# Recurrent branch's projections with 512-column operands, their halves added by VectorE

## The reference, cut to what matters

```python
u = rms_norm(h, norm1_g[l])
proj = (u @ w_in[l]).astype(jnp.float32)
q, k, v, z = jnp.split(proj, [ATTN_WIDTH, 2 * ATTN_WIDTH, 3 * ATTN_WIDTH], axis=-1)
...
prev = jnp.pad(z, ((0, 0), (1, 0), (0, 0)))[:, :-1]
z = z + (prev - z) * shift_mix
```

## Time and profile before

| | us |
|---|---|
| median of 3 runs | 3240.96 (3236.51 to 3246.12) |
| the profiled execution's own time | 3238.11 |
| its span | 3236.3 |
| TensorE busy | 3172.6 |
| VectorE busy | 1626.7 |
| ScalarE busy | 1484.4 |
| GpSimd busy | 2500.0 |

### The profile page before, as it was taken

How to read it: one execution, slowest core, us unless ns; L and a number is a source line. 1 busy time by engine, 2 the same in 40 slices (tenths; PEclk the granted TensorE clock), 3 DMA queues, 4 the chain that set the end, 5 groups by cost and what they waited for, 6 DMA issues and landing times.

```text
span 3236.3 us, 62096 instructions
## 1 busy us (share of the span) xinstructions
PE 3172.6 (98%) x22458; PEld 2810.5 (87%) x22458; DVE 1626.7 (50%) x2999; ACT 1484.4 (46%) x1981; POOL 2500.0 (77%) x1117
## 2 busy tenths in 40 slices
PE   8999999999999999998999999999999999999999
PEld 7888888988888888997789998888888888888888
DVE  3268646522222322497565958876612664157600
ACT  5466544544444444545454554443444335433433
POOL 6821255888888888888587887898898889887887
PEclk9999999999999999999999999999999999999999
DMA  6554204555555555653355555555565555555555
GB/s 223 185 168 127 82 20 134 192 188 189 190 189 189 184 188 185 199 164 124 111 183 170 182 182 174 175 182 175 173 197 188 176 177 186 188 182 175 175 195 169
DMA packets 158763, 553.22 MB, mean 171 GB/s; under 512 B 18000, under 2 KB 24288, under 8 KB 158496
## 3 DMA queue, kind: packets, MB, share of 16 engines
q1 hardware_dynamic: 152208, 541.37, 51.2%
q0 software_dynamic: 3248, 6.77, 0.9%
q10 hardware_dynamic: 3168, 3.15, 0.3%
HBM read 548.33 MB, written 2.88 MB: 170 GB/s over the span
## 4 chain that ended last, share of the span: by engine, by line
PE 66%; POOL 15%; issue 10%; DVE 5%; ACT 2%; DMA 1%; POOLq 0%; ACTq 0%; DVEq 0%; SPq 0%
PE ps L769 37%; PE ps L771 19%; POOL wl L604 15%; PE ps L757 6%; PE ps L1028 1%; DVE wl L1912 1%; PE ps L1340 1%; DVE from_u L2521 1%; ACT wh L1448 0%; DMA xT<-x 0%; PE ps L836 0%; DVE arena L1991 0%; DMA raw<-w_z 0%; ACT under_u L1615 0%; PE ps L955 0%
## 5 line engine op out<-in xcount | busy, mean ns | idle before, releaser
L604 POOL TENSOR_TENSOR wl<-raw,wh 128x1024 fp32r<-128x1024 f32 x980 | 2367.2, 2424 | 482.8 <-ACT wh L1448 480.5
L1448 ACT ACTIVATE wh<-raw 128x1024 fp32r<-128x1024 f32 (+1 forms) x1034 | 1084.2, 1053 | 1415.5 <-PE ps L771 1182.3
L769 PE MATMUL ps<-uhl,wh 128*128 128x512 f32 x3200 | 1119.7, 395 | 12.1 <-DVE uhl L1894 11.7
L771 PE MATMUL ps<-uhl,wl 128*128 128x256 f32 x3200 | 893.0, 279 | 0.0
L769 PEld LDWEIGHTS ps<-uhl,wh 128*128 128x128 f32 x3200 | 600.8, 188 | 149.4 <-DVE wl L1912 10.3
L771 PEld LDWEIGHTS ps<-uhl,wl 128*128 128x128 f32 x3200 | 604.3, 189 | 0.1
L757 PE MATMUL ps<-uhl,wh 128*128 128x256 f32 x2976 | 549.4, 287 | 3.4 <-POOL wl L604 1.2
L769 PE MATMUL ps<-ehl,wh 128*128 128x512 f32 x1536 | 551.4, 400 | 0.3 <-POOL wl L604 0.3
L757 PEld LDWEIGHTS ps<-uhl,wh 128*128 128x128 f32 x2976 | 469.0, 193 | 11.4 <-issue 6.1
L1903 DVE TENSOR_REDUCE ps<-ps 128x256 f32<-128x512 f32 x168 | 117.5, 699 | 634.3 <-PE ps L771 633.5
L771 PE MATMUL ps<-ehl,wl 128*128 128x256 f32 x1536 | 431.6, 281 | 0.0
(11 more groups left out here) (367 smaller groups left out, 3625.7 us busy)
## 6 DMA issues: line engine op xcount, KB each, us to landing
raw<-w_u SPq DMA_DIRECT2D x256, 512.0 KB, 3.7
raw<-w_v SPq DMA_DIRECT2D x256, 512.0 KB, 3.7
raw<-w_gu SPq DMA_DIRECT2D x176, 512.0 KB, 4.3
raw<-w_down SPq DMA_DIRECT2D x80, 512.0 KB, 3.9
raw<-w_out SPq DMA_DIRECT2D x64, 512.0 KB, 3.9
raw<-w_z SPq DMA_DIRECT2D x54, 512.0 KB, 4.2
raw<-w_in SPq DMA_DIRECT2D x52, 512.0 KB, 4.2
raw<-w_qkv SPq DMA_DIRECT2D x48, 512.0 KB, 4.3
```

Source lines behind the costliest of these rows:

```text
L604: pool.tensor_tensor(wl[:, slot, 0:width], raw[:, slot, 0:width], wh[:, slot, 0:width].bitcast(F32), ALU.subtract).then_inc(lo_ready, 1)
L769: pe.matmul(bank(b).rearrange("p (n t) -> p n t", n=2), wh[:, slot, at], both, start=first and c == 0, stop=False, skip_group_check=True)
L771: ins = pe.matmul(bank(b)[:, 0:T], wl[:, slot, at], high, start=False, stop=last and c == kt - 1, skip_group_check=True)
L1448: act.activation(wh[:, slot, 0:width], raw[:, slot, 0:width], ACT.Copy).then_inc(hi_ready, 1)
```

## The change

The tiles of z are computed by `pair_tile`: a 512-column and a 256-column matmul for each chunk. VectorE adds the halves of the bank into a new buffer `ZS` in SBUF (two slots, in `misc`), as the first thing of its turn, ahead of the head's mask. ScalarE's scaled copy and VectorE's shifted product read `ZS`, not the bank. ScalarE waits for the new semaphore `z_sum` instead of for the end of the tile.

```diff
+        ZS = view(misc, 512, 2, T)
...
+        z_sum = sem("z_halves_added")
...
-                    tile(bank(c % 2)[:, 0:T], g, g % RING, uhc, ulc,
-                         (lambda: pe.wait_ge(u_ready, DT)) if c == 0 else
-                         (lambda: key_sums(WT - 1)) if c == 26 else None)
+                    pair_tile(c % 2, g, UHL, (lambda: pe.wait_ge(u_ready, DT)) if c == 0 else
+                              (lambda: key_sums(WT - 1)) if c == 26 else None)
...
-                    act.wait_ge(w_used, BASE["z"] + 2 * c + 2)
+                    act.wait_ge(z_sum, c + 1)
...
-                    act.activation(z_out(c), bank(c % 2)[:, 0:T], ACT.Identity, scale=keep[:, c:c + 1])\
+                    act.activation(z_out(c), ZS[:, c % 2, :], ACT.Identity, scale=keep[:, c:c + 1])\
...
             for c in range(29):
                 h = c - HEAD_LAG
+                if c < 27:
+                    dve.wait_ge(w_used, BASE["z"] + 2 * c + 2)
+                    if c >= 2:
+                        dve.wait_ge(z_ready, c - 1)
+                    add_halves(ZS[:, c % 2, :], c % 2).then_inc(z_sum, 1)
                 if 0 <= h < NH:
                     dve.wait_ge(sc_ps, h + 1)
...
-                    dve.scalar_tensor_tensor(out=late, in0=bank(c % 2)[:, 0:T - 1], scalar=prm("mix", c), in1=late,
+                    dve.scalar_tensor_tensor(out=late, in0=ZS[:, c % 2, 0:T - 1], scalar=prm("mix", c), in1=late,
```

## The result

The changed kernel takes 3245.12 us (median of 22 runs, 3240.61 to 3253.94) where the kernel before, on the same chip in turn with it, takes 3235.89 us (22 runs, 3231.01 to 3246.12). The ratio is 1.0031, with a 95% interval from 1.0025 to 1.0038: some 10 us slower, 8 to 12 us by the interval. The prediction had +9.5 us. Its absolute 3250.5 us lies 5.4 us higher because it started from the three runs shown, whose median is 5.1 us above that of the 22.

A forecast was written before the change was run, and what follows sets the result against it. VectorE together with ScalarE was taken to bound turns 5 to 18. -1.7 (TensorE) + 6.2 (adds) + 3.0 (last turn) + 2.0 (clock) = +9.5 us, a median of 3250.5 us, range 3241 to 3257.

The forecast's parts named there:

- VectorE sets the pace from turn 5 to 18, and two of three adds count: z stage: VectorE with ScalarE paces these turns; nine adds there push the chain, +6.2 us.
- The adds are hidden: Rival, chance 0.10: VectorE's idle time takes the adds in turns 6 to 18; +1.3 us, 3242.3 us.
- The size of an add: VectorE's reduction in the z stage: 0.69 us each, nine adds +6.2 us, lower bound within the mechanism 5.5 us.
- TensorE's gain of 1.7 us: z tiles 3 to 5 and 20, 21, 23, 24, 25: 0.21 us saved a tile on the chain, together -1.7 us.
- -11.8 us: Rival, chance 0.04: TensorE bounds the z stage, all 27 tiles count and slow-clock stretches vanish; 3229.2 us.
- 512-column matmuls much cheaper: Rival, chance 0.03: 512-column matmuls take 0.13 us instead of 0.23, eight tiles gain 13 us more; 3237.5 us.
- The last turn, +3.0: Turn 26: the add waits for the last tile ahead of the key norms, delaying the last bonus sums, +3.0 us.
- The clock, +2.0 with bounds -4.7 and +8: z stage: longer TensorE waits bring 1.2 GHz stretches in turns 10 to 16; turn 19 may give time back.
- no net loss: Rival, chance 0.17: waits pass without slowing TensorE's clock, or turn 19 repays; +7.5 us, 3248.5 us.
- every long wait halves the clock: Rival, chance 0.08: each long TensorE wait brings 1.2 GHz and each delay comes in full; +15.5 us, 3256.5 us.
- everything follows the chain: Behind the z stage: nothing waits for something else that would swallow a delay, so the +9.5 us arrives whole.
- the bound between no change and slower: Total time: a measurement tells about 0.3% from no change, 9.7 us; slower by more had chance 0.44.

The follow-up runs named there:

- pair, no add: Changed kernel without VectorE's adds; readers take the bank's first half, leaving a part out of z: 3238.58 us, ratio 0.9999 to the kernel before.
- adds only: Kernel before, three matmuls a chunk, plus the 27 reductions where the change has them, results unused: 3253.83 us, ratio 1.0037 to the kernel before.
- norms first: Changed kernel with the last key norms ahead of the last add in turn 26: 3246.54 us, ratio 1.0022 to the kernel before.
- turn late, again: The kernel of turn late, unchanged, timed and profiled a second time: 3234.49 us, ratio 0.9991 to the kernel before.
- turn late: Changed kernel reordered: adds behind the maxima, shifted product a turn later, exponentials before z's copy, earlier bank reuse, last norms before last add: 3238.82 us, ratio 0.9999.
- by turn: Changed kernel with 512-column matmuls and adds in turns 0 to 5 and 19 to 25, three matmuls a chunk elsewhere: 3239.84 us, ratio 1.0001.
- kept busy: Changed kernel with 16 unused matmuls ahead of the bonus sums of turns 10, 13, 16 and 19: 3248.27 us, ratio 1.0026.

## Why the prediction came out right, step by step

- **VectorE sets the pace from turn 5 to 18, and two of three adds count: right.** The period grows by 1.22 us with one add and by 1.20 more with two; without adds it is 26.70, and with the adds behind the maxima 26.33 us. *The adds are hidden* is refuted by that; in another place in the queue, behind the maxima, the time is that of before.
- **The size of an add: 0.61 us, not 0.69.** The prediction took the duration, 6.2 us for nine, and named the overlap of rows as its lower bound of 5.5; the lower bound holds: nine times 0.61 is 5.5 us, and 4.9 us of it are seen in the four periods. In this full queue an instruction costs the distance of starts and not its duration.
- **TensorE's gain of 1.7 us: mis-sized, some 1.2.** Tiles 3 to 5 gain 0.38 us (0.65 expected), turns 22 to 25 take 21.85 us instead of 22.37, 0.52 (0.63 expected), in pair, no add 0.40; so 0.13 to 0.17 us a tile instead of 0.21. In the times it is below what can be measured. The two rivals that had TensorE decide (-11.8 us, and 512-column matmuls much cheaper) are refuted: adds only is as slow as the change.
- **The last turn, +3.0: right.** L899 at 3.00 us behind the tile, and 2.9 us back in norms first.
- **The clock, +2.0 with bounds -4.7 and +8: the mechanism right, the cases two.** The waits grew less than expected (2.0, 2.7, at most 2.2, and 1.5 or 3.7, where 2.5, 3.4, 2.5 and 4.3 stood). In the first profile one new stretch costs 0.8 us and turn 19 gives back 4.6; in the second the clock falls behind turns 13 and 19, in tile 26 and in the opening of the recurrence. Both *no net loss* and *every long wait halves the clock* happen, in different executions of one kernel. The sum of the other terms with their measured sizes is -1.2 + 5.5 + 3.0 = +7.3 us; the median's +10 leaves 2.7 us to the clock, a difference that is worked out and not measured by itself. The timed runs have more to say: the twelve shortest of the change average 3243.5 us at a mean granted clock of 0.9934, the ten longest 3250.8 us at 0.9918. All 22 have 0.9927, before's 74 runs in the later sets 0.9946; the difference is some 6 us of TensorE's time (0.0019 of 3240, an estimate), part of which can lie where TensorE has slack.
- **Behind the stage "everything follows the chain": not so.** A delay isn't swallowed there, but stretches take other lengths on their own. One of them may belong to the change: its down projection is 3.1 us shorter in both profiles than before's in both. If that is so in all executions, the stage and the opening of the recurrence lose some 13 us, the clock's part is nearer 6 than 3 us, about what the granted clocks allow at most, and the forecast met the total with two errors that cancel. The runs don't decide this.
- The measured ratio lies where the forecast's middle lay, at the bound between no change and slower that the prediction used. That the total fits to 0.5 us is in part luck: TensorE's gain was 0.5 us too large and the adds 0.7 us too dear, which cancel, and the clock's +2.0 was a choice from a range of 13 us.

## What to carry to other kernels

A busy share of 82% says nothing on whether an engine has room: ask what stands behind the new instruction in its queue, and who waits for that. With the same 27 adds the program takes 10 us more than before when they stand at the head of the turn, and no more than before when they stand behind the maxima, with the copy and the shifted product moved out of their way. An add that stands ahead of something unrelated with a wait of its own, as the last add ahead of the key norms, makes that wait everybody's. And where TensorE must wait for a known time, work that nobody needs can keep the clock up; in one kernel here it brought the next stage forward by 2.7 us, in another the median hardly moved.

## What the runs showed of the hardware that was not expected

**The same wait of TensorE goes either way.** At waits of 1.21 (turn late, again, turn 13), 1.58 (pair, no add), 1.86, 2.29, 2.51, 2.66 and 3.67 us the clock was granted at 1.2 GHz for a time; at 1.22 (turn late, turn 13), 1.31, 1.54, 2.00, 2.69 (the change, turn 13) and 3.00 us (its turn 26) it stayed at 2.4. The change's turn 13, with a wait of 2.69 us in one profile and 2.67 in the other, did both, and so did turn late's with 1.22 and 1.21. So no length of a wait in this range tells by itself which way it goes. The Trainium skill (TensorE: Matmul & The Clock Gate, Part 1 on the clock gate) says that where the clock changes varies from run to run of one kernel; it says so of the start of a kernel, and these traces show it in the middle.

**Stretches of unchanged work take one of two lengths, and only one of them goes with the clock.** From the end of the recurrence to the output projection it is 62.9 or 64.4 us (before once each, the change too). That is the clock: in the three profiles with the short length (before, the change, pair, no add) it is granted at 1.00 from 490 to 560 us, in the ten with the long one at 0.98. Before in its first and second profile:

```profile
490.00:560.00 70.00, 65.37 (x666) 62.07 (x667) 45.77 (x84) 27.82 (x49) 36.77 (x17) 1.00 0.42 136
490.00:560.00 70.00, 65.86 (x627) 62.69 (x624) 44.83 (x82) 28.03 (x48) 35.28 (x16) 0.98 0.42 137
```

The second block's experts take 926.4 or 929.2 us (before 926.4, then 929.2; the change 929.2, then 926.6), at a granted clock of 1.00 from 2200 to 3000 us in every profile. Both change between two executions of one kernel. The 704 chunks of the down projection take 245.3 or 248.4 us, and here each of the three kernels with two profiles kept its length: the change 245.3 in both, before and turn late 248.4 in both; of the others only by turn has the short one. Its 512-column matmuls (ns min/median/max), in the change:

```profile
L771 PE MATMUL ps<-ghl,wh x704: 392/392/397, 1094.9 to 1340.2; 128*128 128x512 f32 x176
```

and in before, the same instructions:

```profile
L769 PE MATMUL ps<-ghl,wh x704: 392/397/398, 1092.0 to 1340.4; 128*128 128x512 f32 x176
```

The median is 392 ns in one and 397 in the other, at a granted clock of 1.00 in both; 704 times 4.4 ns are the 3.1 us. Whether the program decides it (the place of its instructions or buffers) or chance stays open, and nothing was tried on it. Where it is the program, comparisons of two versions by a few us carry it with them: norms first and kept busy have the long one, the change the short one.

**A reduction from PSUM, 128x512 to 128x256, costs its queue 0.60 us** though its row says 0.68. The Trainium skill (VectorE: DVE Perf Modes, the section on the TRN2 errata) has (120 + 512) / 0.96 = 658 ns for it, an estimate by its formula for reads from PSUM; the row's middle is 25 ns longer, the distance of starts some 60 ns shorter.
